# Suffix sums of a stick-breaking attention as pairs of float32r products

## The reference

```python
z = jnp.einsum('bqhd,bkhd->bhqk', q, k) * (HEAD_DIM ** -0.5)
z = z + bias
mask = k_pos[None, :] < q_pos[:, None]
log_keep = jnp.where(mask, jax.nn.log_sigmoid(-z), 0.0)
later = lax.cumsum(log_keep, axis=3, reverse=True) - log_keep
w = jnp.where(mask, jnp.exp(jax.nn.log_sigmoid(z) + later), 0.0)
return jnp.einsum('bhqk,bkhd->bqhd', w, v)
```

## Time and profile before

| | us |
|---|---|
| median of 3 runs | 3793.74 |
| lowest, highest | 3790.5, 3806.12 |
| the profiled execution | 3794.87 |
| its span | 3793.2 |
| PE, DVE, ACT, POOL busy in the span | 3348.2, 1883.2, 1518.0, 1074.2 |
| attention stage | about 886 to 1856 |

### The profile page before, as it was taken

How to read it: one execution, slowest core, us unless ns; L and a number is a source line. 1 busy time by engine, 2 the same in 40 slices (tenths; PEclk the granted TensorE clock), 3 DMA queues, 4 the chain that set the end, 5 groups by cost and what they waited for, 6 DMA issues and landing times. The chain is left out here.

```text
span 3793.2 us, 48151 instructions
## 1 busy us (share of the span) xinstructions
PE 3348.2 (88%) x14713; PEld 2293.3 (60%) x14713; DVE 1883.2 (50%) x2584; ACT 1518.0 (40%) x2479; POOL 1074.2 (28%) x929
## 2 busy tenths in 40 slices
PE   6666767667999999999779979999999999999998
PEld 4444555533444444444268857778777877777777
DVE  5888797894332233323145545534553455345542
ACT  3222423205665666656333334423442344223332
POOL 5999698633333333333101110000000000000000
PEclk8778888778999999999879989999999999999999
DMA  7999798714446654564444543343334333433333
GB/s 248 314 307 300 245 303 263 106 34 121 145 148 174 177 156 146 163 192 148 156 168 138 150 120 97 92 149 104 92 93 151 100 96 104 139 115 124 123 112 113
DMA packets 527291, 590.68 MB, mean 156 GB/s; under 512 B 82457, under 2 KB 338521, under 8 KB 526507
## 3 DMA queue, kind: packets, MB, share of 16 engines
q1 hardware_dynamic: 491704, 562.35, 49.0%
q10 hardware_dynamic: 35224, 25.46, 2.1%
q0 software_dynamic: 176, 0.56, 0.1%
HBM read 525.77 MB, written 61.38 MB: 155 GB/s over the span
## 5 line engine op out<-in xcount | busy, mean ns | idle before, releaser
L2322 PE MATMUL ffn_bank<-ffn_xh,ffn_wh 128*128 128x512 f32 x1408 | 557.9, 396 | 18.6 <-DVE ffn_wl L2536 18.2
L353 POOL TENSOR_TENSOR project_Kr<-project_Kr,project_q_wide 128x1024 f32<-128x1024 f32 x205 | 545.9, 2696 | 65.4 <-DMA project_Kr<-in_cache_k_dram 65.1
L2322 PE MATMUL ffn_bank<-ffn_xl,ffn_wh 128*128 128x512 f32 x1408 | 549.5, 390 | 0.0
L2322 PE MATMUL ffn_bank<-ffn_xh,ffn_wl 128*128 128x512 f32 x1408 | 548.8, 390 | 0.0
L1525 DVE SCALAR_TENSOR_TENSOR att_X<-att_X,att_bank 128x512 f32<-128x512 f32 (+2 forms) x320 | 192.9, 610 | 521.1 <-ACT att_X L1430 520.0
L1385 POOL TENSOR_TENSOR att_S<-att_S,att_X 128x512 f32<-128x512 f32 (+3 forms) x256 | 283.0, 1106 | 339.8 <-PE att_bank L1625 317.9
L2279 POOL TENSOR_TENSOR ffn_st<-ffn_st,kept_eps 128x1 f32<-128x1 f32 x16 | 4.9, 307 | 1216.1 <-ACT ffn_stage L2520 1119.9
L535 DVE TENSOR_REDUCE project_zs<-project_Kr 128x16 f32<-128x1024 f32 x256 | 303.1, 1216 | 84.9 <-POOL project_Kr L353 83.0
L2322 PEld LDWEIGHTS ffn_bank<-ffn_xh,ffn_wh 128*128 128x128 f32 x1408 | 264.9, 188 | 95.2 <-DVE ffn_wl L2536 31.0
L2322 PEld LDWEIGHTS ffn_bank<-ffn_xh,ffn_wl 128*128 128x128 f32 x1408 | 264.9, 188 | 56.4
L2322 PEld LDWEIGHTS ffn_bank<-ffn_xl,ffn_wh 128*128 128x128 f32 x1408 | 265.2, 188 | 52.4
(11 more groups left out here) (360 smaller groups left out, 6116.2 us busy)
## 6 DMA issues: line engine op xcount, KB each, us to landing
project_Kr<-in_cache_k_dram SPq DMA_DIRECT2D x512, 256.0 KB, 4.0
att_Vr<-in_cache_v_dram SPq DMA_DIRECT2D x512, 256.0 KB, 3.4
ffn_wdf<-in_w_down_dram SPq DMA_DIRECT2D x108, 512.0 KB, 3.4
ffn_stage<-in_w_gate_dram SPq DMA_DIRECT2D x89, 512.0 KB, 3.9
ffn_stage<-in_w_up_dram SPq DMA_DIRECT2D x88, 512.0 KB, 4.5
project_w<-in_w_in_dram SPq DMA_DIRECT2D x40, 512.0 KB, 6.0
project_xt<-in_x_prompt_dram SPq DMA_DIRECT2D x16, 512.0 KB
att_qf<-qT_dram SPq DMA_DIRECT2D x64, 128.0 KB, 3.6
```

The source lines that it names most:

```text
L353: pool.tensor_tensor(Kr[:, k % KR], Kr[:, k % KR], q_wide[:, b % 2, None, :].to_broadcast([P, 2, AW]), ALU.mult).then_inc(k_pool, 1)
L2322: mm = pe.matmul(bank[:, first + f % 2, :], w[:, j, k, :], x[:, k, :], start=(k == 0 and n == 0), stop=(k == KD - 1 and n == 2))
```

## The change

The two suffix products are made as float32r products. A float32 tile is written as a rounded part and a rest, both float32r, and each product becomes two: `ones_r` times `Sh` and `Sl` (L1693), `tri_r` times `Xh` and `Xl` (L1697). The constants are float32r copies made once by ACT. The parts come from three engines: ACT rounds the softplus (`round_softplus`, Xh, for unit s-1, at the end of its step), DVE makes its rest (Xl, unit s-2), the rounded running sum (Sh, unit s-2) and the rest of that (Sl, unit s-2), and POOL only sums. `rest_on_pool` is false for every unit, so its branch is never taken. S has three buffers instead of two, and POOL no longer waits for the log-weight product but for the parts of S of three units before. PE waits for `sl_dve` and `xl_ready` where it waited for `s_part` and `sp_ready`. The mask is added by a float32r product.

```diff
-        S = m.sb("S", [P, 2, CH])
+        Xh, Xl = m.sb("Xh", [P, NX, CH], F32R), m.sb("Xl", [P, NX, CH], F32R)
+        S = m.sb("S", [P, NSUM, CH])
+        Sh, Sl = m.sb("Sh", [P, NSUM, CH], F32R), m.sb("Sl", [P, NSUM, CH], F32R)
...
-                        old, new = S[:, (u - 1) % 2, :], S[:, u % 2, :]
-                        pool.wait_ge(logw_ready, b * NU + u)
+                        old, new = S[:, (u - 1) % NSUM, :], S[:, u % NSUM, :]
+                        if u >= NSUM:
+                            v = max(v for v in range(u - NSUM + 1) if carries(v))
+                            pool.wait_ge(sh_ready, b * CARRIES[-1] + CARRIES[v])
+                            if DVE_RESTS[v]:
+                                pool.wait_ge(sl_dve, b * DVE_RESTS[-1] + DVE_RESTS[v])
...
+                def round_softplus(b, u, first):
+                    act.wait_ge(sp_ready, b * NU + u + 1)
+                    if not first or u >= NX:
+                        act.wait_ge(logw_ready, units_to(b, u, NX, first))
+                    act.activation(Xh[:, u % NX, cols(u):], X[:, u % NX, cols(u):], ACT.Copy).then_inc(xh_ready, 1)
...
+                        def rest_of_softplus():
+                            r, u = behind(b, s, 2, first, rest)
...
+                            dve.wait_ge(xh_ready, r * NU + u + 1)
+                            tt(Xl[:, u % NX, o:], X[:, u % NX, o:], Xh[:, u % NX, o:].bitcast(F32), ALU.subtract).then_inc(xl_ready, 1)
...
+                        def rest_of_carry():
+                            r, u = behind(b, s, 2, first, rest)
...
+                            dve.wait_ge(s_part, r * SUMS[-1] + SUMS[u])
+                            if not first or u >= NSUM:
+                                dve.wait_ge(logw_ready, units_to(r, u, NSUM - 1, first))
+                            dve.tensor_copy(Sh[:, u % NSUM, o:], S[:, u % NSUM, o:]).then_inc(sh_ready, 1)
...
+                            dve.wait_ge(sh_ready, r * CARRIES[-1] + CARRIES[u])
+                            tt(Sl[:, u % NSUM, o:], S[:, u % NSUM, o:], Sh[:, u % NSUM, o:].bitcast(F32), ALU.subtract).then_inc(sl_dve, 1)
...
                         if s == 0 or not rest:
                             softplus()
+                        rest_of_carry()
+                        if s <= 1 or not rest:
+                            rest_of_softplus()
...
-                                    pe.matmul(bank[:, s % NZ, o:o + P], ident[:], fillm[:], start=False, stop=False,
+                                    pe.matmul(bank[:, s % NZ, o:o + P], ident_r[:], fill_r[:], start=False, stop=False,
...
-                            pe.wait_ge(sp_ready, r * NU + u + 1)
-                            last = pe.matmul(bank[:, u % NZ, o:], negtri[:], X[:, u % NX, o:], start=False, stop=True,
-                                             skip_group_check=True)
...
-                                pe.wait_ge(s_part, r * SUMS[-1] + SUMS[u - 1])
-                                last = pe.matmul(bank[:, u % NZ, o2:], negones[:], S[:, (u - 1) % 2, o2:], start=False, stop=True,
+                                if rest_on_pool(u - 1):
+                                    pe.wait_ge(sl_pool, r * POOL_RESTS[-1] + POOL_RESTS[u - 1])
+                                else:
+                                    pe.wait_ge(sl_dve, r * DVE_RESTS[-1] + DVE_RESTS[u - 1])
+                                for part in (Sh, Sl):
+                                    pe.matmul(bank[:, u % NZ, o2:], ones_r[:], part[:, (u - 1) % NSUM, o2:], start=False, stop=False,
+                                              skip_group_check=True)
+                            pe.wait_ge(xl_ready, r * NU + u + 1)
+                            for part in (Xh, Xl):
+                                last = pe.matmul(bank[:, u % NZ, o:], tri_r[:], part[:, u % NX, o:], start=False, stop=part is Xl,
                                                  skip_group_check=True)
```

More of the change, by code:

```diff
@@ L1186, in stage_attention @@
     SUMS = [sum(steps(v) for v in range(u + 1)) for u in range(NU)]
+    carries = lambda u: U[u][1] != 0
+    CARRIES = [sum(carries(v) for v in range(u + 1)) for u in range(NU)]
+    rest_on_pool = lambda u: False
+    POOL_RESTS = [sum(carries(v) and rest_on_pool(v) for v in range(u + 1)) for u in range(NU)]
+    DVE_RESTS = [CARRIES[u] - POOL_RESTS[u] for u in range(NU)]
     with ExitStack() as ctx:
@@ L1208, in stage_attention @@
         zero, fillm = m.sb("zero", [P, P]), m.sb("fillm", [P, P])
+        tri_r, ones_r, ident_r, fill_r = (m.sb(n, [P, P], F32R) for n in ("tri_r", "ones_r", "ident_r", "fill_r"))
         Vr = m.sb("Vr", [P, VSLOTS, PP, AW])
@@ L1370, in _, with rest @@
                 pool.wait_ge(consts, 8)
+                def rest(b, u):
+                    o = cols(u)
+                    pool.wait_ge(sh_ready, b * CARRIES[-1] + CARRIES[u])
+                    pool.tensor_tensor(Sl[:, u % NSUM, o:], S[:, u % NSUM, o:], Sh[:, u % NSUM, o:].bitcast(F32), ALU.subtract
+                                       ).then_inc(sl_pool, 1)
                 def sums_round(b):
@@ L1374, in sums_round @@
                         o, x = cols(u), X[:, u % NX, :]
-                        if U[u][1] == 0:
+                        if not carries(u):
+                            if carries(u - 1) and rest_on_pool(u - 1):
+                                rest(b, u - 1)
                             continue
-                        old, new = S[:, (u - 1) % 2, :], S[:, u % 2, :]
-                        pool.wait_ge(logw_ready, b * NU + u)
+                        old, new = S[:, (u - 1) % NSUM, :], S[:, u % NSUM, :]
[4 more added lines that the diff above has]
+                                pool.wait_ge(sl_dve, b * DVE_RESTS[-1] + DVE_RESTS[v])
+                            if POOL_RESTS[v]:
+                                pool.wait_ge(sl_pool, b * POOL_RESTS[-1] + POOL_RESTS[v])
+                        else:
+                            pool.wait_ge(sh_ready, b * CARRIES[-1])
+                            pool.wait_ge(sl_dve, b * DVE_RESTS[-1])
                         pool.wait_ge(sp_ready, b * NU + u + 1)
@@ L1385, in sums_round @@
                             pool.tensor_tensor(new[:, r:], old[:, r:], x[:, r:], ALU.add).then_inc(s_part, 1)
+                        if u and carries(u - 1) and rest_on_pool(u - 1):
+                            rest(b, u - 1)
                 with pool.Fori(0, H) as b:
@@ L1412, in split @@
                     act.activation(qlb[HD:P, cs], wide[HD:P, :], ACT.Copy, scale=bias_now[HD:P, :]).then_inc(b_filled, 1)
+                act.wait_ge(consts, 8)
+                for out, src in ((tri_r, negtri), (ones_r, negones), (ident_r, ident), (fill_r, fillm)):
+                    act.activation(out[:], src[:], ACT.Copy).then_inc(rounded, 1)
                 for c in (3, 2):
                     split(0, c)
+                def round_softplus(b, u, first):
[3 more added lines that the diff above has]
+                    act.activation(Xh[:, u % NX, cols(u):], X[:, u % NX, cols(u):], ACT.Copy).then_inc(xh_ready, 1)
                 def round_(b, steps, first, last, rest):
@@ L1436, in round_ @@
                             act.activation(Wt[:, u % NW, cols(u):], bank[:, u % NZ, cols(u):], ACT.Exp).then_inc(w_ready, 1)
+                        r, u = behind(b, s, 1, first, rest)
+                        if u is not None and not (rest and s > 0):
+                            round_softplus(r, u, first)
                         r, u = behind(b, s, LAG + 2, first, rest)
@@ L1571, in _ @@
                 pe.wait_ge(consts, 8)
+                pe.wait_ge(rounded, 4)
                 def samples_v(b, n):
```

17 lines of the change are left out of this document (14 added, 3 removed).

## The result

The changed kernel takes 3863.44 us (median of 4 runs, 3859.52 to 3875.25), the kernel before on the same chip 3796.64 us (4 runs, 3790.5 to 3806.12): ratio 1.0179, 95% interval 1.0147 to 1.0211. It is slower, by 67 us, and by 22 us more than the 45 that were forecast. The profiled execution of after took 3859.52 us.

A forecast was written before the change was run, and what follows sets the result against it. DVE with POOL in its way at the shared port was taken as the bound, 128.3 us a head against 122.7; 3794.9 plus 45 for 8 heads and a microsecond for rounded constants gives 3841 us, range 3700 to 3950.

The forecast's parts named there:

- The bound moved to DVE with POOL in its way: Attention stage: DVE, blocked by POOL at the shared port, needs 128.3 us a head, above ACT at 98 and PE at 96.
- the signs that the prediction named: New profile: DVE busy over 90%, PE some three quarters, Sl about 1.7 us, POOL sums over 1.3, a head every 128 us.
- Who is let in: Shared port at the CAST's end: waiting POOL goes ahead of DVE's Sl subtraction, which ends 0.55 us after POOL.
- Rivals 2 and 4: 2: DVE keeps the port through three operations, 3760 us, chance 0.12; 4: sums fall into DVE's gaps, 3653 us, chance 0.13.
- The CAST at 0.45: DVE's rounding of the running sum, 512 columns: 0.45 us, and it blocks POOL at the port.
- Rival 3: DVE's CAST stays off the port and takes about 0.69 us; step 3.34 us, kernel 3809 us; chance 0.10.
- A full step of 3.48 us: DVE step with full units: softplus 0.60, CAST 0.45, POOL 1.13, Sl 0.55, Xl 0.72, gap 0.03.
- the end of the sum: Last terms of DVE's full step, behind POOL's end: Sl 0.55, Xl 0.72, gap 0.03 us.
- The rest of a head at 128.3 - 62.6 = 65.7 us: A head outside its 18 plain full steps: DVE's operations laid end to end, without waits, 65.7 us.
- Eight heads at +5.6: Attention stage: each head grows from 122.7 to 128.3 us, +45 us in 8 heads.
- Rival 1: TensorE loses its clock, a quarter of the time at 1.2 GHz, where PE bounds the step: +82 us, 3923; chance 0.20.
- The saving on PE: Suffix products on PE: float32r pairs at 0.45 us instead of 0.86, saving 26 us a head, PE about 96 us.

## Why the prediction was right, and where not

**The bound moved to DVE with POOL in its way: right.** DVE's waits for the logarithm are gone, and PE waits for DVE's rests. Most of the signs that the prediction named came: a mean of 1.53 us for Sl (1.62 to 1.69 where a sum stands in front), 1.32 us for POOL's sums, 0.42 for the CASTs, 0.68 for Xl, 130.7 us a head. Two didn't: DVE is busy for 89% of the stage and not for over 90%, and PE for 82% and not for three quarters. The price was shown by two kernels that take only POOL's part away: 67 us for the sum moved to DVE, 121 us for the sum shortened.

**Who is let in: right.** Sl ends 0.55 us after POOL's end, as the earlier trace rows had it, in step after step (of the 192, 167 are above 1.5 us; 24 have no sum of POOL beside them, and in the one that is left POOL came in behind Sl and made Xl take 1.75 us). The Trainium skill ("SBUF — State Buffer", section on the two separate sides) says of the port pair that VectorE and GpSimd share that whichever of the two starts first has it for its whole instruction, and that the other is blocked until then; Sl at 1.62 us behind POOL's start and at 0.69 without POOL agree with that. Rivals 2 and 4 fall with it: of 168 Sl beside a sum only one takes 0.69 us, and the engines don't miss each other.

**The CAST at 0.45: right.** 0.424 us on average. Rival 3's 0.69 is refuted. Whether the CAST keeps POOL off the port is not shown: POOL's sum is recorded from 0.84 us after the start of the softplus and not from 0.77, and takes 1.32 instead of 1.29 us. The question is worth some 0.1 us a step.

**A full step of 3.48 us: too long by 0.24.** It measured 3.24. The step that failed is the end of the sum, 0.55 + 0.72 + 0.03 behind POOL's end. The subtraction for Xl starts 0.08 us before Sl has ended (1345.40 against 1345.48), and the softplus 0.60 us after Xl: together 1.07 us from POOL's end (1344.93) to the next softplus, not 1.30. The 0.72 of the earlier trace rows belongs to the subtraction for k, which works on 64 rows, and it keeps that distance in the changed kernel (1508.73 to 1509.45); the 0.60 of the earlier trace rows is what back-to-back operations of 128 rows and 512 columns really cost, for two SBUF inputs too. For the 18 plain steps that makes 58.3 us where 62.6 were counted.

**The rest of a head at 128.3 - 62.6 = 65.7 us: too short by 6.7.** The other 22 steps took 130.7 - 58.3 = 72.4. They were counted as DVE's operations laid end to end, without waits. In fact 13 of them take 46.1 us, with DVE busy for 37.89 us of the 45.65 of one head. The waits that had been put at nothing are DVE's for the copies of q and k on ACT (2.7 us in step 36 and 3.5 in step 1) and the turn of the loop (some 2 us); spreading the copies took 2.9 us off a head. The rest stays open. The two errors have opposite signs and leave 2.4 us a head in heads 2 to 7.

**Eight heads at +5.6: the first one mis-sized.** This is most of what the forecast missed. The gap to 122.7 was taken from starts that lie in step 31 of each head, and used for the first head too. That head took 102.1 us before and grew by 22.6, which is 17 us over the forecast; heads 2 to 7 grew by 7.5 each, 11 over it; the last by 2.0, 4 under it. A bound that is the same for every head has to be set against each head's own length.

**Rival 1, the clock.** The granted clock fell to 0.91 in the stage, as the rival said, for 21 of a head's 131 us. But with the same low clock the sum on DVE took back all 67 us, and the full steps kept 3.24 us with more or less work on PE. So the mechanism of the case, PE as the bound at 1.2 GHz, didn't come. What the lower clock can have cost is small: some 2 us a head in the last nine steps, by the estimate from the heads above, where the case had 10 a head.

**The saving on PE.** The pair products came at the forecast price: 0.23 us from start to start where PE is at its full clock (1349.00, 1349.23, 1349.46, 1349.69), 0.42 to 0.43 at the lower one (1345.34, 1345.77, 1346.20, 1346.62):

```profile
1345.77 0.63 PE L1693 MATMUL att_bank<-att_Sh,att_ones_r 128*128 128x512 f32 x1
...
1346.20 0.63 PE L1693 MATMUL att_bank<-att_Sl,att_ones_r 128*128 128x512 f32 x1
...
1349.23 0.39 PE L1693 MATMUL att_bank<-att_Sh,att_ones_r 128*128 128x512 f32 x1
...
1349.46 0.40 PE L1693 MATMUL att_bank<-att_Sl,att_ones_r 128*128 128x512 f32 x1
```

## What to carry to other kernels

An operation that is moved to an engine costs what that engine's port neighbour is doing, not only its own time: look for the rows where the two meet, and count the neighbour's whole instruction into the step. Do a change of two halves one at a time, since the half that stays under the next engine's limit may win what the whole loses. And set a new bound against every stretch of the loop by itself, the first round and the steps with side work too: a stretch that keeps its length in every variant is not held by the engine that was made faster. Look also at what else such a stretch holds, engine by engine: once-a-head work on the engine that has become full costs its whole length.

## What was not expected of the hardware

- Back-to-back DVE operations of 128 rows and 512 columns start 0.60 to 0.61 us apart while each is recorded with 0.67 to 0.69 us, with two SBUF inputs as well as with one from PSUM. Records overlap by 0.08; spacing is what a step costs. The two subtractions for q and k, of 64 rows each, start 0.71 to 0.72 us apart and don't overlap.
- POOL's sum in front of one DVE subtraction costs a step 0.95 us, less than the 1.32 us that it lasts, since it is recorded as starting before the CAST has ended; DVE makes the same sum in 0.60.
- 3.4 us at the lower clock cost 1.4 to 1.6 us where PE set the pace, and nothing in steps that DVE set.
- At a turn of the loop over heads DVE and ACT of the changed kernel stand for some 2 us without a wait that the profile shows.
